# A two-layer diffusion trunk on one core: the first quarter of a value projection moved in behind the norm, with four staging slots

## The reference

```python
hl = modulate(rmsnorm(xl, mix_norm_g[1]), sh1, sc1)      # latent tokens
hc = modulate(rmsnorm(xc, mix_norm_g[1]), mc[0], mc[1])  # context tokens

qkv = hl @ w_qkv                                         # w_qkv: 1024 x 3072
to_grid = lambda t: t.reshape(B, rows, GRID_W, H, dh).transpose(0, 3, 1, 2, 4)
qg, kg, vg = to_grid(qkv[..., :D]), to_grid(qkv[..., D:2 * D]), to_grid(qkv[..., 2 * D:])
kv_c = hc @ w_qkv[:, D:]
```

## Time and profile before

| what | value |
|---|---|
| median of 3 runs | 3200.8 us (3199.91 to 3202.48) |
| profiled execution | 3199.34 us, span of its instructions 3197.5 us |
| mean granted TensorE clock | 0.974 of full speed |
| TensorE busy | 2978.2 us, 93% of the span |
| VectorE, ScalarE, GpSimd busy | 1762.4, 814.8 and 737.0 us |
| value projection, first and last matmul | 1633.1 and 1759.8 us |

### The profile page before, as it was taken

How to read it: one execution, slowest core, us unless ns; L and a number is a source line. 1 busy time by engine, 2 the same in 40 slices (tenths; PEclk the granted TensorE clock), 3 DMA queues, 4 the chain that set the end, 5 groups by cost and what they waited for, 6 DMA issues and landing times.

```text
span 3197.5 us, 44615 instructions
## 1 busy us (share of the span) xinstructions
PE 2978.2 (93%) x15738; PEld 2467.4 (77%) x15738; DVE 1762.4 (55%) x2975; ACT 814.8 (25%) x1425; POOL 737.0 (23%) x457
## 2 busy tenths in 40 slices
PE   5899999689999999999969899999798999999996
PEld 1588888478888888888759788888675888888884
DVE  1645545666666776655551366666614554555556
ACT  1311111321111111111142366666623111111112
POOL 0221111021111111111111254445421222222210
PEclk8899999899999999999989999999998999999998
DMA  9210013021222212211035556555630111111111
GB/s 356 73 53 26 32 46 89 0 69 55 76 72 74 79 55 78 69 44 39 33 95 123 166 144 177 161 160 144 182 138 26 39 52 46 40 59 39 59 39 59
DMA packets 156872, 269.26 MB, mean 84 GB/s; under 512 B 70272, under 2 KB 97920, under 8 KB 156800
## 3 DMA queue, kind: packets, MB, share of 16 engines
q1 hardware_dynamic: 156800, 268.32, 26.8%
HBM read 222.13 MB, written 50.07 MB: 85 GB/s over the span
## 4 chain that ended last, share of the span: by engine, by line
PE 77%; DVE 6%; issue 5%; ACT 4%; DMA 4%; SPq 1%; POOL 1%; DVEq 0%; POOLq 0%; ACTq 0%
PE psum L668 42%; PE psum L699 19%; PE psum L828 4%; PE psum L807 3%; PE psum L882 2%; PE psum L851 2%; PE psum L865 2%; DMA o_dram<-o_st_lo 1%; DVE residual L1343 1%; DVE prod L1323 1%; DMA mod_raw<-mod_panels 1%; PE psum L634 1%; POOL w_lo L1657 1%; ACT squares L982 1%; ACT pt_hi L1158 1%
## 5 line engine op out<-in xcount | busy, mean ns | idle before, releaser
L1343 DVE SCALAR_TENSOR_TENSOR residual<-psum,modulation,residual 128x512 f32<-128x512 f32 (+1 forms) x1072 | 718.2, 690 | 884.5 <-PE psum L699 882.5
L1657 POOL TENSOR_TENSOR w_lo<-raw,w_hi 128x1024 fp32r<-128x1024 f32 x196 | 491.2, 2520 | 1927.9 <-ACT w_hi L976 1925.0
L668 PE MATMUL psum<-act_hi,w_hi 128*128 128x512 f32 (+1 forms) x2208 | 589.2, 367 | 9.5 <-POOL w_lo L1657 7.5
L668 PE MATMUL psum<-act_lo,w_hi 128*128 128x512 f32 (+1 forms) x2208 | 589.3, 367 | 0.0
L668 PE MATMUL psum<-act_hi,w_lo 128*128 128x512 f32 (+1 forms) x2208 | 588.7, 367 | 0.0
L668 PEld LDWEIGHTS psum<-act_hi,w_hi 128*128 128x128 f32 x2208 | 397.7, 188 | 88.3 <-issue 7.7
L976 ACT ACTIVATE w_hi<-raw 128x1024 fp32r<-128x1024 f32 x196 | 204.1, 1061 | 1013.8 <-PE psum L668 938.1
L668 PEld LDWEIGHTS psum<-act_lo,w_hi 128*128 128x128 f32 x2208 | 380.2, 188 | 70.7
L668 PEld LDWEIGHTS psum<-act_hi,w_lo 128*128 128x128 f32 x2208 | 380.3, 188 | 70.5
L699 PE MATMUL psum<-prod_hi,w_hi 128*128 128x512 f32 (+1 forms) x1072 | 408.3, 381 | 28.2 <-DVE residual L1343 10.4
L699 PE MATMUL psum<-prod_hi,w_lo 128*128 128x512 f32 (+1 forms) x1072 | 396.3, 370 | 0.0
(11 more groups left out here) (120 smaller groups left out, 3707.4 us busy)
## 6 DMA issues: line engine op xcount, KB each, us to landing
raw<-ffn_panels SPq DMA_DIRECT2D x132, 512.0 KB, 5.0
mod_raw<-mod_panels SPq DMA_DIRECT2D x48, 512.0 KB, 9.6
mod_in<-mod_rest SPq DMA_DIRECT2D x64, 384.0 KB, 3.1
raw<-conv_panels SPq DMA_DIRECT2D x32, 512.0 KB, 5.2
k_hi<-k_dram SPq DMA_DIRECT2D x32, 320.0 KB, 5.7
k_lo<-k_dram SPq DMA_DIRECT2D x32, 320.0 KB, 7.3
v_st<-v_dram SPq DMA_DIRECT2D x32, 320.0 KB, 7.2
raw<-qk_panels SPq DMA_DIRECT2D x16, 512.0 KB, 4.4
```

The source lines that it names most:

```text
L668: mm = pe.matmul(psum[:, bank + b, 0:tn], w[:, s, kb, :], acts[h][:, kb, t0:t0 + tn], start=(kb == 0 and n == 0), stop=(kb == KB - 1 and n ...
L1343: dve.scalar_tensor_tensor(out=residual[:, ob, t0:t0 + tn], in0=psum[:, 6 + r % 2, 0:tn], scalar=modulation[:, gates + ob, kind_of(t0):kin ...
L1657: pool.tensor_tensor(panel(w_lo, s), raw[:, s], panel(w_hi, s), ALU.subtract).then_inc(lo_done[s], 1)
```

## The change

The first quarter is no longer computed piece by piece. `v_behind_norm` walks norm 2 batch by batch and block by block; as soon as a block's low part is there it multiplies that block for the four pieces of the batch (two in batch 2), each in its own bank. The half sums and the fold of the next batch stand behind blocks 1, 3 and 5. Pieces 0 and 1 are drained inside batch 1 behind block 1, pieces 2 and 3 behind block 2, pieces 4 to 7 at the same places in batch 2 (`V_BEHIND`). The stages get four slots each. The split of panel slots 2 and 3 on ScalarE stands behind `v_high(8)` instead of `v_high(4)`. The other three quarters are as before.

```diff
+V_STAGES = 4
-        stage_v_hi, _ = place("stage_v_hi", [P, 2, 2 * P], F32, scratch_at)
-        stage_v_lo, _ = place("stage_v_lo", [P, 2, 2 * P], F32, scratch_at + 4 * T)
+        stage_v_hi, _ = place("stage_v_hi", [P, V_STAGES, 2 * P], F32, scratch_at)
+        stage_v_lo, _ = place("stage_v_lo", [P, V_STAGES, 2 * P], F32, scratch_at + 4 * T)
...
+        V_BEHIND = {(1, 1): (0, 1), (1, 2): (2, 3), (2, 1): (4, 5), (2, 2): (6, 7)}
...
+            def v_products(n, kb, quarter):
+                t = n % TOK_TILES
+                for part, (h, w) in enumerate(((act_hi, w_hi), (act_lo, w_hi), (act_hi, w_lo))):
+                    mm = pe.matmul(psum[:, V_BANKS[n % 4], 0:2 * P], h[:, kb, t * P:(t + 1) * P],
+                                   w[:, 2 * quarter:2 * quarter + 2, kb, :],
+                                   start=(kb == 0 and part == 0), stop=(kb == KB - 1 and part == 2))
+                if kb == KB - 1:
+                    mm.then_inc(v_ready, 1)
+            def v_behind_norm():
+                for s in (0, 1):
+                    pe.wait_ge(lo_done[s], base["v"][s] + 1)
+                for b, (t0, tn) in enumerate(ALL):
+                    for kb in range(KB):
+                        wait_lows(pe, norms[2], b * KB + kb)
+                        for n in range(t0 // P, (t0 + tn) // P):
+                            if kb == 0:
+                                pe.wait_ge(v_lo_done, n + 1)
+                            v_products(n, kb, 0)
+                        if b + 1 < len(ALL):
+                            if kb in (1, 3):
+                                norm_half(2, ALL, b + 1, kb // 2)
+                            elif kb == 5:
+                                norm_fold(2, ALL, b + 1)
             def v_quarter(i, quarter):
...
-                    if n * P % BANK == 0 and n < TOK_TILES:
-                        b = n * P // BANK
-                        if b == 0:
-                            norm_sums(2, ALL, 1)
-                        wait_lows(pe, norms[2], b * KB + KB - 1)
...
-                    if n in (1, 2):
-                        norm_half(2, ALL, 2, n - 1)
-                    elif n == 3:
-                        norm_fold(2, ALL, 2)
...
+            v_behind_norm()
+            v_quarter(0, 1)
+            v_quarter(1, 0)
+            v_quarter(1, 1)
...
-            def first_v(b):
-                if b == 1:
-                    for n in range(4):
-                        v_high(n)
+            def first_v(b, kb):
+                for n in V_BEHIND.get((b, kb), ()):
+                    v_high(n)
...
-                    if n >= 4:
+                    if n >= 8:
                         v_high(n)
-                    if t == TOK_TILES // 2 - 1:
+                    if t == (8 if quarter == 0 else TOK_TILES // 2 - 1):
                         for s in ((2, 3) if quarter % 2 == 0 else (0, 1)):
                             split_hi("v", s, (quarter + 1) // 2)
```

More of the change, by code:

```diff
@@ L237, in trunk @@
         v_ready, v_hi_done, v_lo_done = sem("v_ready"), sem("v_hi_done"), sem("v_lo_done")
-        v_out = [sem("v_out0"), sem("v_out1")]
+        v_out = [sem(f"v_out{n}") for n in range(V_STAGES)]
         qk_ready, qk_hi_done, qk_lo_done = sem("qk_ready"), sem("qk_hi_done"), sem("qk_lo_done")
@@ L446, in store_v @@
                         sp.dma_start(v_dram[h0:h0 + 4, :, t, part].rearrange("h p d -> p h d"),
-                                     stage[:, t % 2].rearrange("p (h d) -> p h d", d=DH)).then_inc(v_out[t % 2], 16)
+                                     stage[:, n % V_STAGES].rearrange("p (h d) -> p h d", d=DH)
+                                     ).then_inc(v_out[n % V_STAGES], 16)
                     if t == TOK_TILES // 2 + 1:
@@ L509, in _ @@
                 store_qk(0, n)
-            for n in range(2):
-                sp.wait_ge(v_out[n], 16 * 4 * TOK_TILES)
+            for n in range(V_STAGES):
+                sp.wait_ge(v_out[n], 32 * 4 * TOK_TILES // V_STAGES)
             sp.wait_ge(hi_done[2], base["qk"][2])
@@ L798, in v_quarter @@
                     n = (2 * i + quarter) * TOK_TILES + t
-                    if n * P % BANK == 0 and n < TOK_TILES:
-                        b = n * P // BANK
-                        if b == 0:
-                            norm_sums(2, ALL, 1)
-                        wait_lows(pe, norms[2], b * KB + KB - 1)
                     pe.wait_ge(v_lo_done, n + 1)
                     for kb in range(KB):
[L806 to L810, removed]
-                    if n in (1, 2):
-                        norm_half(2, ALL, 2, n - 1)
-                    elif n == 3:
-                        norm_fold(2, ALL, 2)
-            for i in range(2):
-                v_quarter(i, 0)
-                v_quarter(i, 1)
+                        v_products(n, kb, quarter)
+            v_behind_norm()
+            v_quarter(0, 1)
+            v_quarter(1, 0)
+            v_quarter(1, 1)
             def qk_matmuls(i, tile, bank, lo, hi):
@@ L995, in norm_root, with norm @@
                                scale=1.0 / (COL_TILE * D)).then_inc(norms[n].rooted, 1)
-            def norm(n, tiles, ready=None, after=None):
+            def norm(n, tiles, ready=None, behind=None):
                 m = norms[n]
@@ L1030, in norm @@
                             high(b, kb)
+                        if behind is not None:
+                            behind(b, kb)
                         if fused and b + 1 < len(tiles):
@@ L1039, in norm @@
                                 norm_root(n, tiles, b + 1)
-                    if after is not None:
-                        after(b)
             act.wait_ge(consts, CONSTS)
@@ L1108, in v_high @@
                 act.wait_ge(v_ready, n + 1)
-                at_least(act, v_out[n % 2], 32 * (n // 2))
-                act.activation(stage_v_hi[:, n % 2].bitcast(F32R), psum[:, V_BANKS[n % 4], 0:2 * P],
+                at_least(act, v_out[n % V_STAGES], 32 * (n // V_STAGES))
+                act.activation(stage_v_hi[:, n % V_STAGES].bitcast(F32R), psum[:, V_BANKS[n % 4], 0:2 * P],
                                ACT.Copy).then_inc(v_hi_done, 1)
-            def first_v(b):
-                if b == 1:
-                    for n in range(4):
-                        v_high(n)
+            def first_v(b, kb):
+                for n in V_BEHIND.get((b, kb), ()):
+                    v_high(n)
             norm(2, ALL, lambda b: act.wait_ge(ffns[0].added, done * (HIDDEN - 1) + KB * (b + 1) + 2), first_v)
@@ L1297, in _, with norm @@
             norm_scales(0)
-            def norm(n, tiles, after=None):
+            def norm(n, tiles, behind=None):
                 m = norms[n]
@@ L1473, in v_low, with first_v @@
             def v_low(n):
-                at_least(dve, v_out[n % 2], 32 * (n // 2))
+                at_least(dve, v_out[n % V_STAGES], 32 * (n // V_STAGES))
                 dve.wait_ge(v_hi_done, n + 1)
[L1476 to L1482, removed]
+                dve.tensor_tensor(stage_v_lo[:, n % V_STAGES].bitcast(F32R), psum[:, V_BANKS[n % 4], 0:2 * P],
+                                  stage_v_hi[:, n % V_STAGES], ALU.subtract).then_inc(v_lo_done, 1)
+            def first_v(b, kb):
+                for n in V_BEHIND.get((b, kb), ()):
+                    v_low(n)
             norm(2, ALL, first_v)
-            for n in range(4, 4 * TOK_TILES):
+            for n in range(8, 4 * TOK_TILES):
                 v_low(n)
```

## The result

| | before | after |
|---|---|---|
| median of 5 runs | 3200.53 us (3199.09 to 3202.48) | 3213.83 us (3212.98 to 3216.35) |
| profiled execution, span | 3199.34, 3197.5 us | 3216.25, 3214.3 us |
| mean granted clock | 0.974 | 0.968 |

The ratio after to before is 1.0044 (95% interval 1.0033 to 1.0054). The forecast was 3213.7.

A forecast was written before the change was run, and what follows sets the result against it. TensorE's solid run of matmuls was taken to bound the kernel, so piece 10's start decides. Terms (a) to (d), 4.3 + 3.8 + 3.2 + 1.6 = 12.9 us, on the 3200.8 median give 3213.7; range 3205 to 3220.

The forecast's parts named there:

- (a): Norm 2, batches 0 and 1 to batch 2's first scaling: half sums behind products make it 48.13 us against 43.79, +4.3.
- the twin: Norm 1 in the old trace, where `project_behind_norm` already walks block by block; its times were used to price norm 2.
- (b): Block 0 of batch 1: TensorE waits for PSUM banks to be drained, delaying batch 2's half sum by 2.7 to 4.9, taken as 3.8.
- (c): Batch 2's first scaling to piece 10, which waits for the uncovered panel split: 18.4 us against 15.2, +3.2 (to 4.0).
- (d): TensorE's restart at piece 10 after some 6 us of waiting: low clock for the first 17 matmuls, +1.6 us.
- (e): Quarters 2 to 4: TensorE never waits for a store there today, so four slots win nothing.
- The norm did not keep its pace: Rival: half sums not delayed behind products, (a) and (b) take 40.5 us instead of 51.9; total 3202.3, chance 0.08.
- The panels were not in time: Rival: something other than the split releases piece 10, so its wait and slow restart go; total 3205.9, chance 0.06.
- Both together: Rival: the norm keeps its pace and the panels are in time; total 3194.5, chance 0.02.
- The low clock did not last: Rival: all of norm 2's batches 0 and 1 run at half speed, +8.3 us more; total 3222, chance 0.10.
- the pattern named for it: Trainium skill's warning for the low-clock rival: bursts shorter than the waits between them each start slow again, giving 3222.

The follow-up runs named there:

- experiment 2: Changed kernel with each half sum and fold of the next batch ahead of the products of blocks 0, 3 and 5 in TensorE's queue: 3202.9 us.
- experiment 5: Changed kernel with pieces 0 and 1 drained behind block 0 of batch 1 and pieces 2 and 3 behind block 1, a block earlier: 3209.4 us.
- experiment 1: Changed kernel with weight panels 2 and 3 split early, inside batch 0 of the norm behind the high part of block 2: 3205.2 us.
- (4): Kernel before with only the split of weight panels 2 and 3 moved from behind the high drain of piece 4 to that of piece 8: 3209.2 us.
- experiment 6: Changed kernel with both the early split of panels 2 and 3 and the sums ahead of the products: 3196.8 us.
- experiment 3: Kernel before with four staging slots for the value results instead of two, nothing else: 3199.4 us.

## Why the prediction was right, step by step

**(a) Batches 0 and 1 by the twin, +4.3.** Batch 0 took 26.0 us from first scaling to first scaling (1614.58 to 1640.58). The first half sum started at 8.0 us; the twin said 7.83. With the sums first the first half sum came at 4.34 and batch 0 took 22.2 (experiment 2): shown. Batch 0 stayed 1.9 longer than in the kernel before (20.2).

**(b) The wait for banks, +3.8 of 2.7 to 4.9.** The half sum of batch 2 started 9.85 us after the first scaling of batch 1, in norm 1 5.6 (631.85 against 626.23, the first scaling of its batch 1): 4.2 late. But the batch ended only 2.8 late (24.8 us against 22.0), since norm 1 had itself lost about that difference to the low clock later in its batch 1, in block 3 and the sum behind it:

```profile
635.89 0.71 PE L685 MATMUL psum<-act_hi,w_hi 128*128 128x512 f32 x1 [1.88 <-POOL act_lo L1666]
...
638.66 0.98 PE L634 MATMUL psum<-squares,ones 128*32 128x256 f32 x8
```

That is 2.8 us from block 3 to its sum; in the changed kernel it was 1.6 (1654.46 to 1656.09). With (a), 50.8 us came out where 51.9 had been forecast: the term was 1.1 too large. The sign and the place of the wait hold (experiment 5). Its price does not stand by itself: 2.8 us against the twin, 4.6 when the sums were moved ahead of it (batch 1 in experiment 2), 0.4 when only the banks were freed earlier.

**(c) Batch 2 up to piece 10, +3.2 forecast, +3.5 measured.** 11.35 us to the last low part (11.0 forecast), 7.3 from there to piece 10 (7.4 forecast). No row stood behind the 0.15 us for the wake-up; 0.10 was measured, from 1683.96 to 1684.06. That the split is uncovered is shown twice, by taking it away (1) and by putting it alone into the old kernel (4).

**(d) The restart at half clock, +1.6.** 3.62 us for 17 matmuls, as at 1653.07. It went together with the wait in experiment 1, and in experiment 6 the granted clock of the solid stretch rose from 0.98 to 1.00.

**(e) Nothing later.** TensorE had no wait in the last three quarters, in both kernels.

**The sum** for the stage was 12.9; it measured 12.0: 7.0 for (a) and (b) together, 3.5 for (c) and 1.5 for (d). That the median came out at 13.3, next to the forecast of 13.2 over the same before, is partly luck: in the profiled pair the unchanged rest behind the first query load took 1442.4 us after and 1437.7 before. In the ten kernels, whose code from there on is the same, this rest lies between 1436.2 and 1442.6.

**The rivals.** The norm did not keep its pace; with the sums first it took 42.4 us and the kernel 3202.9 (experiment 2), near the 40.5 and 3202.3 of this rival. The panels were not in time, and experiment 1 gives what that would have brought (3205.2, where the rival said 3205.9). Both together were put at 3194.5 and measured 3196.8. The low clock did not last: 0.83 in both batches. Nor did the pattern named for it occur, bursts of 1.4 us between waits of 2 to 4: in batch 0 TensorE worked for 8.1, 4.3, 2.5 and 4.5 us, with waits of 2.27, 0.58 and 3.46 between. So this run does not test a rule for bursts that are shorter than the waits. In the rival's sum the upper end of (b) lies 1.1 above 3.8, not 0.9, which moves it by 0.2 us.

**A reading that was off.** The 5.6 us of drains before batch 2 count from 1652.6, but that is the first low drain; the first high drain began at 1650.4. Of the time before batch 2 the four slots took away 4.4 us (experiment 3). The +4.3 of (a) does not rest on this, as it compares the whole of two norms; the 40.5 of the first rival does.

## What to carry to other kernels

Where work is moved in behind a producer, look at what stood in the old order for free. Here the sums that feed the producer came to stand behind the consumer's products, and a weight split lost the two pieces that had covered it; together they turned a change that is worth some 4 us without them (experiment 6) into a loss of 13. Short work that another engine waits for goes ahead of long work that nobody waits for yet, and a split goes where its engine waits anyway. If the same pattern already runs elsewhere in the kernel, its trace is a good price list for the new place.

## What the runs showed of the hardware

TensorE restarted at half clock with the same figure in both kernels: 3.61 us for 17 matmuls of piece 4 before (1653.07, after 4.97 idle) and 3.62 for 17 of piece 10 after (1684.06, after 5.84 idle). After a shorter wait of 3.46 us, at 1638.38 in the changed kernel, it began at full clock: behind the first gap of 0.22 the starts came 0.12 us apart up to 1639.69, and only from there, while it was working, 0.21 apart. In the middle of the norm the same code met the low clock at different places from kernel to kernel, and a gain of 1.7 us shrank to 0.4 that way (experiment 5). Stages with unchanged code moved too: the first scaling of norm 2 came between 1608.9 and 1615.3 us in the ten profiles, a spread as large as most effects looked for here. Lengths of some 50 us measured from S agreed to 0.1 us where the code in them was the same or its edit lay in a wait (43.8 and 43.8; 50.8 and 50.8), while the 1440 us behind the stage spread over 6.4. For a change of a few us, the stage's own length told more than the medians.
